# Dropping the wait for the second block's gathered rows ahead of the load of the fourth fixed expert's first weight matrix

## What is computed

```python
def hier_moe(h, w_rg, b_rg, w_re, b_re, w1, w3, w2):
    # router: one group of 4, then 2 of its 8 experts, for each of the 1024 rows
    ...
    x_pad = jnp.concatenate([xf, jnp.zeros((1, D), xf.dtype)], axis=0)
    xb = x_pad[slot_tok].reshape(NB, MOE_BLOCK, D)      # rows gathered by expert

    def expert_block(args):
        xi, e = args
        return (jax.nn.silu(xi @ w1[e]) * (xi @ w3[e])) @ w2[e]

    yb = lax.map(expert_block, (xb, block_e)).reshape(P, D)
    yb = (yb * slot_w[:, None]).astype(h.dtype)
    out = jnp.zeros((T + 1, D), h.dtype).at[slot_tok].add(yb)[:T]   # scattered back and added
```

## Time and profile before

| | us |
|---|---|
| median of 3 runs | 1471.84 (1471.55 to 1472.11) |
| the profiled execution, its time | 1471.9 |
| its span, first to last instruction | 1470.0 |
| PE busy in the span | 1426.6 (97%) |
| DVE / ACT / POOL busy | 629.1 / 334.7 / 110.2 |
| DMA read and written | 277.47 MB and 20.09 MB |

### The profile page before, as it was taken

How to read it: one execution, slowest core, us unless ns; L and a number is a source line. 1 busy time by engine, 2 the same in 40 slices (tenths; PEclk the granted TensorE clock), 3 DMA queues, 4 the chain that set the end, 5 groups by cost and what they waited for, 6 DMA issues and landing times. The chain is left out here.

```text
span 1470.0 us, 20298 instructions
## 1 busy us (share of the span) xinstructions
PE 1426.6 (97%) x8154; PEld 697.2 (47%) x8154; DVE 629.1 (43%) x1276; ACT 334.7 (23%) x673; POOL 110.2 (7%) x145
## 2 busy tenths in 40 slices
PE   7999999999999999999999999999989899999997
PEld 4445457787876565444444444433323233333332
DVE  4498445646474357553635455752110111111111
ACT  3613332323236352111110222301010111111110
POOL 2000000000000100000000001001111111111111
PEclk9999999999999999999999999999999999999999
DMA  9790200111112101112104842799999999999995
GB/s 360 258 367 1 66 0 1 29 29 29 29 29 58 29 1 43 43 29 58 39 19 172 319 196 98 266 387 405 414 408 406 404 363 403 405 414 404 405 413 160
DMA packets 80285, 292.55 MB, mean 199 GB/s; under 512 B 13408, under 2 KB 42302, under 8 KB 61505
## 3 DMA queue, kind: packets, MB, share of 16 engines
q1 hardware_dynamic: 73634, 274.51, 47.5%
q0 software_dynamic: 6560, 16.77, 4.5%
HBM read 277.47 MB, written 20.09 MB: 202 GB/s over the span
## 5 line engine op out<-in xcount | busy, mean ns | idle before, releaser
L794 PE MATMUL PS<-R 128*32 128x512 f32 (+4 forms) x3637 | 653.7, 567 | 21.6 <-POOL R L652 9.1
L794 PE MATMUL PS<-HT,R 128*32 128x512 f32 (+1 forms) x1576 | 424.2, 599 | 4.2 <-DMA R<-in_expert_w 4.2
L794 PEld LDWEIGHTS PS<-R 128*32 128x32 f32 (+2 forms) x3637 | 235.0, 127 | 324.6 <-issue 298.5
L794 PEld LDWEIGHTS PS<-HT,R 128*32 128x32 f32 (+1 forms) x1576 | 149.9, 139 | 196.1 <-issue 194.6
L794 PE MATMUL PS<-R,HT 128*128 128x512 f32 (+1 forms) x672 | 234.0, 503 | 2.9 <-ACT R L1569 1.5
L1950 DVE TENSOR_TENSOR R<-R,PS 128x512 f32<-128x512 f32 (+1 forms) x86 | 66.1, 779 | 343.8 <-PE PS L794 343.7
L1569 ACT ACTIVATE R<-PS 128x512 f32<-128x512 f32 (+3 forms) x116 | 69.5, 610 | 451.7 <-PE PS L794 290.4
L794 PEld LDWEIGHTS PS<-R,HT 128*128 128x128 f32 x672 | 125.0, 190 | 93.7 <-issue 80.2
L794 PE MATMUL PS<-WK,R 128*32 128x512 f32 (+1 forms) x440 | 96.8, 600 | 0.0
L1958 DVE SCALAR_TENSOR_TENSOR R<-PS,R,gate 128x1024 f32<-128x1024 f32 (+1 forms) x23 | 28.5, 1238 | 127.7 <-PE PS L794 121.2
L752 POOL DMA_INDIRECT out_rows<-R x36 | 52.3, 1453 | 300.6 <-DVE R L1958 151.1
(11 more groups left out here) (275 smaller groups left out, 935.3 us busy)
## 6 DMA issues: line engine op xcount, KB each, us to landing
R<-in_expert_w SPq DMA_DIRECT2D x38, 2048.0 KB, 26.6
R<-in_expert_w SPq DMA_DIRECT2D x48, 1024.0 KB, 14.4
HT<-in_expert_w SPq DMA_DIRECT2D x15, 2048.0 KB
R<-in_ada_w SPq DMA_DIRECT2D x16, 1024.0 KB, 5.0
HT<-in_expert_w SPq DMA_DIRECT2D x16, 1024.0 KB, 14.8
WK<-in_expert_w SPq DMA_DIRECT2D x7, 2048.0 KB, 23.9
R<-in_w_in SPq DMA_DIRECT2D x24, 512.0 KB, 4.6
R<-in_ada_w SPq DMA_DIRECT2D x16, 512.0 KB, 10.6
```

The lines of the kernel that those rows point to most:

```text
L794: return nc.tensor.matmul(o, l, r, start=a, stop=z)
```

## The change

SP no longer waits on L572 for the semaphore of the second gather. Nothing else differs; every engine has the same instructions in the same order, and line numbers behind it are lower by one.

```diff
@@ -569,7 +569,6 @@
             for u in range(2):
                 e.wait_ge(xn_st[u], 16 + 16 * NT // 2)
             e.wait_ge(s["rt_mm"], 2 + NT)
-            e.wait_ge(xg_ld[1], 16)
             load_ew(0, 3, FIXED[3])
```

## The result

| | us |
|---|---|
| before, median of 6 runs | 1471.69 (1471.34 to 1473.32) |
| after, median of 6 runs | 1477.38 (1476.12 to 1479.58) |
| ratio after / before, 95% interval | 1.0034 (1.0024 to 1.0045) |
| the profiled executions: time, span | before 1471.9, 1470.0; after 1476.88, 1475.0 |
| PE busy in the span | before 1426.6, after 1430.8 |

The kernel became slower by 5.7 us; the ratio says 3.5 to 6.6. The forecast was 1474.1 with a range from 1471.6 to 1476.6: the sign was forecast, the size was too small, and the time lies outside the range. The predicted wait of PE was there, nearly to the number. What took the time past the range stood in rival (b), with a price that was too low.

A forecast was written before the change was run, and what follows sets the result against it. PE sets the time in general, sharing it with DMA from the expert stage on. Load moved 0 plus PE's gather wait 2.2 us, on the profiled 1471.9, gives 1474.1; range 1471.6 to 1476.6.

The forecast's parts named there:

- rival (b): PE behind its wait for block 1's gather: the clock falls too, costing 1.7 us more, 1475.8; chance 0.20.
- The load moves forward and gains nothing: Load (0, 3) on SP: first half issued near 945.1 instead of 951.66, gain 0; (1, 3) still waits for PE.
- The gather lands near 955.2 and PE waits 2.2 us: Block 1's gather, issued at 947.66, lands behind load (0, 3); PE waits before the transposes from 953.1, 2.2 us.
- rival (c): Block 1's gather as late as under the full stream, 955.8 to 957.3; PE waits 2.7 to 4.2 us; about 1475.4; chance 0.20.
- One for one to the end: PE's 2.2 us delay puts (1, 3) at 960.5; the four later load waits keep their length and come 2.2 us later.
- Rival (a): Block 1's gather passes the DMA engines in one go, landing at 952.9 before PE asks; 1471.9, no change; chance 0.11.
- (d): The earlier load pulls later loads forward by 2.0 us, shrinking the wait that ends at 1162.96; 1469.9; chance 0.07.

The follow-up runs named there:

- the second trace: The changed kernel, with nothing further changed, measured and profiled again: 1476.73 us beside 1472.09 us for the kernel before, ratio 1.0032.
- pure delay in the kernel before: 16 needless 128x128 matmuls on PE ahead of the transposes of block 1, added to the kernel before: 1476.5 us beside 1472.51, ratio 1.0026.
- The filled wait at 1163: 12 needless 128x128 matmuls ahead of the second half of up(9), added to the kernel before: 1472.52 us beside 1472.44, ratio 1.0001.
- the kernel whose gather stood ahead of the load: Against the kernel before, SP waits for the table of block 2, not the landed gather; first set 1475.3 us beside 1472.51, ratio 1.0016.

## Why the prediction was wrong, point by point

- **The load moves forward and gains nothing: right.** It was issued at 946.24 rather than 945.1 and nothing else came earlier. (1, 3) was still issued at PE's word.
- **The gather lands near 955.2 and PE waits 2.2 us: right in the wait, late in the landing.** It began to move 4.3 us after its issue (4.2 in the working), and PE waited 2.51, 2.17 in the second trace. But PE started at 956.18 and 955.56, and a start past 955.8 was the sign of rival (c), a gather as late as under the full stream. The first trace has that sign. It doesn't have (c)'s wait of 2.7 us or more, since PE itself came to this place at 953.67 and not at 953.09. With (c)'s own 1475.4 the time would still not be reached.
- **One for one to the end: right.** 4.93 us at (1, 3), 5.22 at 1168, 5.0 at the end; and 3.6 us of pure delay in the kernel before came out as 4.0 in the median. The waits for loads were not quite as long as before: 11.6 us in three in place of 13.1 in four, 12.9 in the second trace. The filled wait at 1163 corrects the reason. The reading behind it was that in the 137 us without a wait behind 1163 only PE sets the time. Yet faster by 2.4 us it meets a late load at 1435: DMA has less than that to spare. So a delay of the stream passes to the end, since it delays PE and the loads, and in this trace a gain of PE alone did not.
- **The clock: the step that failed.** The sum had nothing for it. It stood as rival (b) with a chance of 0.20, at 1.7 us, "nearly all the time at 1.2 GHz" over little more than 3 us. Measured are 6.8 us of low clock, of which 4.8 with PE at work, so 2.4 us. The chance rested on the question whether 2.2 us of idling suffice, which the rows left open; 1.08 us did, and in one trace 0.47, while 0.32 in another did not. With 2.5 and 2.4 us the sum would have been 1476.8. The longer price was there to be read: the second of the earlier trace rows, 0.53 over 5.0 us, is 2.4 us, and I took the smaller one. The range then ended at 1476.6, below the two terms together.
- **Rival (a), the gather in one go: fell.** By (a) it would have been through 1.0 us after 951.9. PE got it at 956.18, and until 955 the packets of q0 stood beside those of q1: 20.3% of the engines' time for q0 and 79.6% for q1 over 3.6 us. The one case in which it passed early is the kernel whose gather stood ahead of the load. The rule of the Trainium skill on which (a) leaned (DMA: Bandwidth & Descriptors, Queues, rings and completion order: a whole group of descriptors from one queue before the engine turns) is neither shown nor refuted by this. The rows add up 16 engines, and groups that pass on each engine at another time would look spread out as well. The same holds for the prediction's reading of the earlier trace rows.
- **(d), the stream pulled forward: fell.** The hole moved to 956 to 964 and grew.

## What to carry to other kernels

A wait that holds back a transfer nobody needs yet can be what keeps a small, urgent transfer ahead of it; look at what shares the engines in the microseconds after it, and who waits with how little slack. Price a stall of PE as its length plus the half-speed work behind it, and put both terms in the main case where the rows show half the clock behind other stalls. Whether the small matmuls ahead of this one had a part in it was not tested. And before taking out a stall for a gain, look for the resource that is next late: here, where DMA and PE were both full, it was less than 2.4 us away.

## What the runs showed of the hardware

An idle time of PE of 1.08 us behind the matmuls of `rank_rows()` went with a granted clock of 1.2 GHz for 3.4 us, one of 2.10 us with 6.8 us of it (clock of 953 to 963: 0.83 and 0.66). The length of the idle time alone does not tell how long: 0.47 and 1.69 us also went with 3.4 us (0.83), 0.32 us with none (1.00), and the 3.92 us of the earlier trace rows with no more than the 3 us of the earlier trace rows, since the clock of 1103 to 1108 was 1.00 again. Nearly the same stretch filled with needless 128x128 matmuls kept 1.00 with a rest of 0.20 us of waiting. An indirect gather issued 0.4 us ahead of a load of SP was overtaken by it, and one issued 1.4 us ahead was not (one trace each); behind a standing load its first packet came 4.3 us after the issue, where in the kernel before, with the load held back, it came in less than 2 (issue at 947.66, packets from 949 on).
